# Second block of a three-block model: two PSUM banks and buffers for the attention's turned probabilities and results, the scan in two banks with its products grouped by kind, three of the head norms placed between attention tiles

## Chip, cores and metric

The kernel runs on one core of one Trainium2 chip. The metric is device time in microseconds of one execution; lower is better.

## The reference

Three transformer blocks follow each other on a sequence of 512 positions of width 1024. Only the mixing of the second block is touched. It is, shortened:

```
h = rmsnorm(x, attn_norm); p_nsa, p_rw, p_moba = split(h @ w_in)
o_nsa  = head_rmsnorm(nsa_mixer(p_nsa), nsa_out_gain)     # 6 heads of 64: compressed, selected and window attention, gated
o_rw   = rwkv7_mixer(p_rw)                                # 4 heads of 64: a linear recurrence with a 64x64 state per head
o_moba = head_rmsnorm(moba_mixer(p_moba), moba_out_gain)  # 6 heads of 64: attention over chosen blocks
x = x + concat(o_nsa, o_rw, o_moba) @ w_out
```

`head_rmsnorm` divides each head's 64 numbers by their root mean square and multiplies by a gain.

## The kernel before, in words

Every activation lies in SBUF with features on the 128 partitions and tokens along them, so that 128 features are a tile of 128 x 512. Weights come in units of 1024 x 128. TensorE multiplies them in three passes (line 573), because ScalarE and VectorE split each weight unit and each input into a high and a low part.

The work is written as stages. Each stage is a set of generators, one for each engine, and each generator yields a planned time before it issues a few instructions. `weave` merges the generators of an engine by these times, so the planned times fix the order of instructions in each engine's queue, and semaphores do the rest. Planned times are in units; a unit of the plan is the time of one weight unit. A stage's time that comes earlier or later in the plan changes only the order.

In the second block 26 units of projections (`Projected`, two lines of 17 and 9 units) fill the tiles P2. A unit's result stands in PSUM bank 6 or 7, and VectorE evicts it (line 962). Beside and after them run:

- `PairCausal`, the attention of both kinds. Its 36 steps each treat one tile of 128 queries for a pair of heads (m = 0, 1), against up to four tiles of 128 keys. The first 24 steps belong to the first attention (two steps to a result tile), the other 12 to the second (one step to a result tile), in all 24 result tiles. A step: scores on TensorE (line 1696) into banks 0 and 1; mask and minimum on VectorE (line 1753); exponential on ScalarE (line 1777); reciprocal and scaling on VectorE (lines 1760 to 1764); a turn for each m, in which TensorE transposes the probabilities in tiles of 128 x 128 into bank 2 (line 1713) and ScalarE copies them to the buffer PT (line 1785); weighing of the values on TensorE (line 1724, line 1728 for the compressed part, whose probabilities are turned by line 1711 and copied by line 1787) into bank 3; and after a tile's last step a copy of the result by ScalarE (line 1792). Bank 2 and PT are single, or one half for each m: the second turn waits for the first copy, the copies of a step wait for the weighing of the step before.
- `RwkvScan`, the recurrence in 16 chunks of 32 positions, a chunk each 1.45 units, from unit 26.4. The positions of chunk c lie on the 32 partitions (c mod 4). A chunk's products, for four heads each: x from the tokens (line 1425) and from the state (line 1445), VectorE's copy with a minus sign (line 1492), u (line 1458), its copy (line 1496), the state's increment (lines 1452 and 1467) and the state's update on VectorE (lines 1488 and 1500), and the result from state (line 1429), tokens (line 1430) and u (line 1434), copied by ScalarE (line 1509). The result's products from state and tokens alternate head by head, two heads before and two after the second half of the state's increment. x stands in banks 4 and 5, u in 4, the state's increment in bank 6, the result in bank 7.
- `RwkvOutput`, after the scan, normalises its result (lines 1812 to 1845).
- `HeadMeans`, six norms of a 128 x 512 tile of attention results: a square on ScalarE (line 1870), a product with a matrix of ones on TensorE (line 1891), logarithm and exponential on ScalarE (lines 1879 and 1880), each with a table load ahead of it, and a product on VectorE (line 1898). All six are planned after the scan, from 1.5 units after it on, 0.3 units apart, with two buffers and banks 4 and 5.

After them the output projection of the block begins, again with line 573, and needs all norms.

The two lines that give the order of turns and copies in the plan before:

```
x.turned = [max([x.after[0] + 0.12] + ([last.keep[1] + 0.08, last.out + 0.05] if s else []))]
x.turned.append(max(x.after[1] + 0.12, x.keep[0] + 0.08))
```

Of the kernel before, what the change touches and what calls it, by code (L numbers as in the profile page):

```python
# [41 lines left out]
CH = 32  # L42

# [892 lines left out]
class Projected(Line):  # L936


    def __init__(self, core, n, at, dst, func=ACT.Copy, bias=None, inputs=None, before=None, sums=None, eighth=()):
        super().__init__(core, n, at, WHOLE, (6, 7), inputs)  # L940
# [453 lines left out]
class RwkvScan(Stage):  # L1394
# [17 lines left out]
    def tensor(self, pe):  # L1412
# [23 lines left out]
        yield self.when(0) - 0.3  # L1436
        pe.wait_ge(self.rwkv.kept.sem, self.rwkv.kept.at(12))
        pe.wait_ge(self.compress.kept.sem, self.compress.kept.at(2))
        x_first(0)
        for c in range(n):  # L1440
            t0, d = self.when(c), self.step
            yield t0
            pe.wait_ge(self.s_kept.sem, self.s_kept.at(c + 1))
            for h, (lo, t, o, r) in enumerate(heads):
                last = pe.matmul(x_bank(c, h, t), AR[lo:lo + 64, t, c, 0], STATE[lo:lo + 64, c % 2, t], start=False, stop=(t == 1))
            last.then_inc(self.x_ready.sem, 1)
            if c:
                out_last(c - 1)
            if c == 0:
                pe.wait_ge(self.proj.free.sem, self.proj.free.at(N2))  # L1450
            for lo, t, o, r in heads:
                pe.matmul(s_bank(lo, t), tok(c)[1][:, o:o + 64], tok(c)[2][:, o:o + 64], start=(t == 0), stop=False)
            yield t0 + 0.33 * d
# [2098 lines left out]
```

## Time and profile before

| what | value |
|---|---|
| median of 3 runs | 2953.69 us (2952.72 to 2962.31) |
| profiled execution, its own time | 2959.89 us |
| its span, first to last instruction | 2958.1 us |
| mean granted TensorE clock | 0.928 of full speed |
| TensorE busy | 2768.2 us, 94% |
| VectorE busy | 1521.9 us, 51% |
| ScalarE busy | 1058.2 us, 36% |
| GpSimd busy | 313.1 us, 11% |

Busy times are of one profiled execution. TensorE's products are pipelined and their ends are modelled, so the step from one start to the next tells more than the duration of one. The granted clock has two levels, 1.2 and 2.4 GHz, shown as 0.5 and 1; a mean between them is a share of time at each.

### The profile page before, as it was taken

The numbers are of one execution on the slowest core, as the hardware profiler recorded it, in microseconds if no ns is written. First come the engines' busy times: TensorE is split into PE (matmuls) and PEld (weight loads), VectorE is DVE, ScalarE is ACT, GpSimd is POOL, SyncE is SP. The second block draws the span as 40 slices with busy tenths as digits, with TensorE's granted clock in tenths as the row PEclk, the third lists the DMA queues.
The fourth block names the chain that finished last, engine by engine and source line by source line (L and its number), as shares of the span: only waits on it lengthen the run. The fifth ranks groups of instructions, "written<-read, shape, count | busy, mean of one in ns | idle before, by whom it ended". The sixth has DMA issues, their size and how long they took to land.

```text
span 2958.1 us, 36434 instructions
## 1 busy us (share of the span) xinstructions
PE 2768.2 (94%) x14774; PEld 2203.9 (75%) x14774; DVE 1521.9 (51%) x2473; ACT 1058.2 (36%) x1831; POOL 313.1 (11%) x220
## 2 busy tenths in 40 slices
PE   7999999999999999988869999998899899899998
PEld 6778888999997767655636777776666568678886
DVE  3786643544445463733334787544753453533444
ACT  3365444442223332322264222343332332322322
POOL 0043210012220100000001222020000000100001
PEclk8999999999999999955568999999989999999999
DMA  3211111223332413200003665332121123223332
GB/s 117 72 44 51 58 58 58 74 84 93 93 93 93 136 57 101 77 1 1 1 1 100 199 199 188 97 118 68 58 64 57 36 62 95 86 86 93 95 98 71
DMA packets 70852, 239.06 MB, mean 81 GB/s; under 512 B 12212, under 2 KB 13109, under 8 KB 70430
## 3 DMA queue, kind: packets, MB, share of 16 engines
q1 hardware_dynamic: 63054, 208.88, 23.0%
q10 hardware_dynamic: 7632, 27.86, 2.8%
q8 instruction: 118, 1.93, 0.3%
q14 instruction: 48, 0.39, 0.0%
HBM read 234.06 MB, written 2.64 MB: 80 GB/s over the span
## 4 chain that ended last, share of the span: by engine, by line
PE 62%; DVE 11%; ACT 4%; issue 3%; POOL 1%; ACTq 0%; DVEq 0%; POOLq 0%
PE ps L573 49%; DVE wl L364 2%; PE ps L1713 1%; PE ps L2656 1%; PE ps L1696 1%; ACT wh L358 1%; PE ps L1724 1%; PE ps L3307 1%; DVE xl L654 1%; DVE arena L3000 1%; PE ps L1429 1%; DVE arena L1032 1%; PE ps L1430 1%; PE ps L1572 0%; ACT arena L1785 0%
## 5 line engine op out<-in xcount | busy, mean ns | idle before, releaser
L573 PE MATMUL ps<-xh,wh 128*128 128x512 f32 (+1 forms) x2728 | 1022.8, 389 | 39.0 <-DVE xl L679 14.8
L573 PE MATMUL ps<-xl,wh 128*128 128x512 f32 (+1 forms) x2728 | 995.5, 379 | 0.0
L573 PE MATMUL ps<-xh,wl 128*128 128x512 f32 (+1 forms) x2728 | 991.4, 378 | 0.0
L364 DVE TENSOR_TENSOR wl<-ring,wh 128x1024 fp32r<-128x1024 f32 x374 | 471.1, 1260 | 657.0 <-ACT wh L358 655.9
L358 ACT ACTIVATE wh<-ring 128x1024 fp32r<-128x1024 f32 x374 | 395.3, 1057 | 998.8 <-PE ps L573 891.1
L573 PEld LDWEIGHTS ps<-xh,wh 128*128 128x128 f32 x2728 | 504.6, 191 | 179.7 <-issue 56.8
L573 PEld LDWEIGHTS ps<-xl,wh 128*128 128x128 f32 x2728 | 503.0, 190 | 101.2 <-issue 9.6
L573 PEld LDWEIGHTS ps<-xh,wl 128*128 128x128 f32 x2728 | 504.2, 191 | 99.4
L734 POOL TENSOR_TENSOR arena<-arena 128x512 f32<-128x512 f32 (+1 forms) x42 | 72.0, 1721 | 1899.2 <-ACT arena L718 1899.2
L1952 PE MATMUL ps<-xh,wh 128*128 128x264 f32 (+1 forms) x816 | 260.1, 319 | 9.6 <-DVE xl L423 9.6
L1952 PE MATMUL ps<-xh,wl 128*128 128x264 f32 (+1 forms) x816 | 234.9, 288 | 0.0
L1952 PE MATMUL ps<-xl,wh 128*128 128x264 f32 (+1 forms) x816 | 234.9, 288 | 0.0
L1952 PEld LDWEIGHTS ps<-xh,wh 128*128 128x128 f32 x816 | 157.3, 193 | 38.4 <-issue 20.7
L1952 PEld LDWEIGHTS ps<-xl,wh 128*128 128x128 f32 x816 | 158.3, 194 | 1.0
L1952 PEld LDWEIGHTS ps<-xh,wl 128*128 128x128 f32 x816 | 157.9, 194 | 0.0
L818 DVE TENSOR_TENSOR h<-ps,h 128x512 f32<-128x512 f32 (+1 forms) x64 | 44.3, 692 | 155.6 <-PE ps L573 155.6
L875 POOL TENSOR_TENSOR arena<-arena 128x516 f32<-128x516 f32 (+1 forms) x44 | 81.0, 1842 | 217.5 <-ACT arena L854 217.5
L862 ACT ACTIVATE arena<-arena 128x512 f32<-128x512 f32 x44 | 27.8, 632 | 203.2 <-DVE arena L894 203.2
L1753 DVE CUSTOM_DVE_ANT_0 arena<-ps,con 128x128 f32<-128x128 f32 (+3 forms) x72 | 33.2, 488 | 115.8 <-PE ps L1696 84.1
L820 DVE SCALAR_TENSOR_TENSOR h<-ps,mod,h 128x512 f32<-128x512 f32 x40 | 30.0, 751 | 113.5 <-PE ps L573 113.5
L1713 PE MATMUL ps<-con,arena 128*128 128x128 f32 x180 | 52.0, 409 | 31.7 <-ACT arena L1785 22.3
L878 POOL TENSOR_TENSOR arena<-arena 128x512 f32<-128x512 f32 x44 | 58.4, 1327 | 159.4 <-ACT arena L862 159.4
(391 smaller groups left out, 3010.8 us busy)
## 6 DMA issues: line engine op xcount, KB each, us to landing
ring<-in_weights SPq DMA_DIRECT2D x374, 512.0 KB, 3.6
arena<-in_w_ada ACTq DMA_DIRECT2D x48, 512.0 KB, 4.6
arena<-in_cmp_w SPq DMA_DIRECT2D x2, 2048.0 KB
h<-in_x ACTq DMA_DIRECT2D x4, 528.0 KB, 6.6
arena<-strip_scratch SPq DMA_DIRECT2D x8, 264.0 KB, 3.7
out_features<-arena SPq DMA_DIRECT2D x8, 256.0 KB, 2.1
con<-in_consts SPq DMA_DIRECT2D x1, 777.0 KB, 11.0
arena<-in_c ACTq DMA_DIRECT2D x1, 512.0 KB, 3.8
```

The lines of the kernel that those rows point to most:

```text
L358: act.activation(flat(self.wh[:, s % 2]), flat(self.ring[:, s % RING]), ACT.Copy).then_inc(self.hi_ready, 1)
L364: dve.tensor_tensor(flat(self.wl[:, s % 2]), flat(self.ring[:, s % RING]), flat(self.wh[:, s % 2]).bitcast(F32), ALU.subtract).then_inc(se ...
L573: last = pe.matmul(self.place(u, e), w[:, k, :], x[:, k, o:o + m], start=(k == 0 and i == 0), stop=(k == self.chunks - 1 and i == 2))
L654: ins = dve.tensor_tensor(xl, a, xh, ALU.subtract)
L734: pool.tensor_tensor(self.acc, self.sq[:, 0] if k == 1 else self.acc, self.sq[:, k % 2], ALU.add).then_inc(self.added.sem, 1)
L818: ins = dve.tensor_tensor(out, self.got(u), out, ALU.add)
L820: ins = dve.scalar_tensor_tensor(out=out, in0=self.got(u), scalar=self.scale[u], in1=out, op0=ALU.mult, op1=ALU.add)
L875: pool.tensor_tensor(g, g, self.r_gate, ALU.mult).then_inc(self.gate_scaled.sem, 1)
L878: pool.tensor_tensor(self.mid[:, j, 2], self.mid[:, j, 2], self.r, ALU.mult).then_inc(self.scaled.sem, 1)
L1713: last = pe.transpose(ps[:, 2, j * P:(j + 1) * P], self.X[:, s % 3, m, j * P:(j + 1) * P], ident)
L1753: dve.tensor_tensor_reduce(out=self.X[:, s % 3, m, 0:nk], in0=core.ps[:, m, 0:nk], in1=core.c("causal")[:, DIAG - x.i * P:DIAG - x.i * P + ...
L1952: last = pe.matmul(self.place(e), w[:, k, :], x[:, k, o:o + m], start=(k == 0 and n == 0), stop=(k == NC - 1 and n == 2))
```

## The change

Five edits in one:

1. The attention's turned probabilities stand in bank 2 for m = 0 and in bank 6 for m = 1, and PT has two buffers, one for even and one for odd steps (the second on the tiles MV and MV + 1). The second turn no longer waits for the first copy; the copies of step s wait for the weighing of step s - 2. The plan puts both turns before both copies.
2. Result tiles alternate between banks 3 and 7.
3. The scan uses banks 4 and 5 alone and starts at unit 26.6. x of each chunk is made in one visit, both kinds; the state's increment is one run of products after u; the result is one run of products after it, by kind (tokens, u, state). x waits for ScalarE's copy of the result before. The copy of x is two instructions. Its plan has other shares of the chunk.
4. The norms of the first attention are planned right after their tiles, in bank 7, those of the second from 1.8 units after the scan's end on in bank 5, at least 0.8 units apart, with one buffer each for square and root (on the tiles NG and MV + 2). Result tiles 5, 9 and 13 wait for the logarithm of a norm.
5. The second line of projections uses banks 5 and 4.

```diff
+SCAN_STEP = 1.45
...
-        x_bank = lambda c, h, t: core.ps[rows(c), 4 + h % 2, t * 64:t * 64 + 64]
-        s_bank = lambda lo, t: core.ps[lo:lo + 64, 6, 256 + t * 64:256 + t * 64 + 64]
-        o_bank = lambda c, lo, t: core.ps[lo:lo + 64, 7, t * CH:(t + 1) * CH]
+        x_bank = lambda c, h, t: core.ps[rows(c), 4 + h % 2, 256 * (h % 2) + 64 * t:256 * (h % 2) + 64 * t + 64]
+        u_bank = lambda c, r: core.ps[rows(c), 4, 64 * r:64 * r + 64]
+        s_bank = lambda lo, t: core.ps[lo:lo + 64, 4, 256 + t * 64:256 + t * 64 + 64]
+        o_bank = lambda lo, t: core.ps[lo:lo + 64, 5, t * CH:(t + 1) * CH]
...
-        def out_first(c, some):
-            for lo, t, o, r in some:
-                pe.matmul(o_bank(c, lo, t), STATE[lo:lo + 64, c % 2, t], AR[lo:lo + 64, t, c, 1], start=(t == 0), stop=False)
-                pe.matmul(o_bank(c, lo, t), tok(c)[2][:, o:o + 64], parts(c)[:, r, 1, 1], start=False, stop=False)
-
-        def out_last(c):
+        def state(c):
+
+            for e, F in ((1, lambda o, r: tok(c)[2][:, o:o + 64]), (0, lambda o, r: U[rows(c), 64 * r:64 * r + 64])):
+                for lo, t, o, r in heads:
+                    last = pe.matmul(s_bank(lo, t), tok(c)[e][:, o:o + 64], F(o, r), start=(e == 1 and t == 0), stop=(e == 0 and t == 1))
+            last.then_inc(self.s_ready.sem, 1)
+
+        def out(c):
             for lo, t, o, r in heads:
-                last = pe.matmul(o_bank(c, lo, t), U[rows(c), 64 * r:64 * r + 64], parts(c)[:, r, 0, 1], start=False, stop=(t == 1))
+                pe.matmul(o_bank(lo, t), tok(c)[2][:, o:o + 64], parts(c)[:, r, 1, 1], start=(t == 0), stop=False)
+            for lo, t, o, r in heads:
+                pe.matmul(o_bank(lo, t), U[rows(c), 64 * r:64 * r + 64], parts(c)[:, r, 0, 1], start=False, stop=False)
+            for lo, t, o, r in heads:
+                last = pe.matmul(o_bank(lo, t), STATE[lo:lo + 64, c % 2, t], AR[lo:lo + 64, t, c, 1], start=False, stop=(t == 1))
             last.then_inc(self.o_ready.sem, 1)
...
             pe.wait_ge(self.s_kept.sem, self.s_kept.at(c + 1))
+            if c:
+                pe.wait_ge(self.o_kept.sem, self.o_kept.at(c))
+            else:
+                pe.wait_ge(self.rwkv.kept.sem, self.rwkv.kept.at(12))
+                pe.wait_ge(self.proj.free.sem, self.proj.free.at(N2))
+            x_first(c)
...
-            dve.tensor_scalar(self.X[rows(c)].rearrange("p (o n) -> p o n", o=2), core.ps[rows(c), 4:6, 0:128], -1.0, None,
-                              ALU.mult).then_inc(self.x_kept.sem, 1)
+            for e in range(2):
+                ins = dve.tensor_scalar(self.X[rows(c), 128 * e:128 * e + 128], core.ps[rows(c), 4 + e, 256 * e:256 * e + 128], -1.0, None,
+                                        ALU.mult)
+            ins.then_inc(self.x_kept.sem, 1)
...
-            x.turned = [max([x.after[0] + 0.12] + ([last.keep[1] + 0.08, last.out + 0.05] if s else []))]
-            x.keep = [x.turned[0] + 0.1]
-            x.turned.append(max(x.after[1] + 0.12, x.keep[0] + 0.08))
-            x.keep.append(x.turned[1] + 0.1)
-            x.weigh = x.keep[1] + 0.1
+            x.turned = [max([x.after[0] + 0.12] + ([last.keep[0] + 0.08] if s else []))]
+            x.turned.append(max([x.after[1] + 0.12, x.turned[0] + 0.06] + ([last.keep[1] + 0.08] if s else [])))
+            x.keep = [max(x.turned[0] + 0.12, last.keep[1] + 0.04 if s else 0)]
+            x.keep.append(max(x.turned[1] + 0.12, x.keep[0] + 0.08))
+            x.weigh = max(x.keep[1] + 0.14, last.weigh + 0.05 if s else 0)
...
+    def bank(self, s):
+        return 3 + 4 * (self.tiles[s] % 2)
+
+    def room_for(self, pe, s):
+        t = self.tiles[s]
+        if t >= 2:
+            pe.wait_ge(self.out_used.sem, self.out_used.at(t - 1))
+        if t in (5, 9, 13):
+            pe.wait_ge(self.means.logs.sem, self.means.logs.at(t // 4))
...
-            if s or m:
-                pe.wait_ge(self.kept.sem, self.kept.at(2 * s + m))
-            else:
+            if s:
+                pe.wait_ge(self.kept.sem, self.kept.at(2 * s + m - 1))
+            elif m == 0:
                 self.room(pe)
...
-                last = pe.transpose(ps[:, 2, j * P:(j + 1) * P], self.X[:, s % 3, m, j * P:(j + 1) * P], ident)
+                last = pe.transpose(ps[:, 2 + 4 * m, j * P:(j + 1) * P], self.X[:, s % 3, m, j * P:(j + 1) * P], ident)
...
-                if s:
-                    act.wait_ge(self.weighed.sem, self.weighed.at(s))
-                else:
+                if s >= 2:
+                    act.wait_ge(self.weighed.sem, self.weighed.at(s - 1))
+                elif s == 0:
                     self.room_kept(act)
-                ins = act.activation(self.PT[:, m, 0:nk], ps[:, 2, 0:nk], ACT.Copy)
+                ins = act.activation(self.PT[s % 2][:, m, 0:nk], ps[:, 2 + 4 * m, 0:nk], ACT.Copy)
...
+        for n, (t, x, gain, ready, bank, room) in enumerate(self.items):
+            yield t
+            ready(act)
+            if n:
+                act.wait_ge(self.summed.sem, self.summed.at(n))
+            act.activation(self.sq, x, ACT.Square).then_inc(self.squared.sem, 1)
+            yield t + 0.4
+            act.wait_ge(self.summed.sem, self.summed.at(n + 1))
+            if n:
+                act.wait_ge(self.applied.sem, self.applied.at(n))
+            act.activation(self.r, core.ps[:, bank, :], ACT.Ln, bias=core.c("eps6"), scale=1.0 / 64).then_inc(self.logs.sem, 1)
+            act.wait_ge(self.logs.sem, self.logs.at(n + 1))
+            act.activation(self.r, self.r, ACT.Exp, scale=-0.5).then_inc(self.root.sem, 1)
...
-    PT = core.area(NKC * T, 2, T)
+    PT = [core.area(t * T, 2, T) for t in (NKC, MV)]
...
-                               eighth=[a - u + t for a in (NQ, MQ) for t in range(3)]))
+                               eighth=[a - u + t for a in (NQ, MQ) for t in range(3)], banks=(5, 4) if u else (6, 7)))
...
-        free = max(free + 0.3, x.out + 0.1)
+        free = max(free + 0.8, x.out + 0.02 if n < 3 else max(x.out + 0.1, scanned + 1.8))
```

## Rows read from the trace of the kernel before

**Rows 1.** Stage windows: us, busy time of each engine, granted clock, DMA share
```profile
1250.00:1496.00 246.00, 221.26 (x1589) 148.02 (x1587) 81.38 (x308) 63.83 (x201) 0.00 (x0) 0.53 0.01 3
...
1504.60:1541.20 36.60, 17.58 (x64) 8.38 (x64) 11.78 (x33) 33.91 (x49) 0.00 (x0) 0.72 0.00 0
```
**Rows 2.** TensorE's groups by line, 1250 to 1496 us: busy, mean ns, idle before
```profile
L1713 PE MATMUL ps<-con,arena 128*128 128x128 f32 x136 | 40.9, 425 | 8.6 <-ACT arena L1785 6.2 <-DVE arena L1762 2.4
L1696 PE MATMUL ps<-arena 64*128 64x384 f32 (+3 forms) x108 | 39.7, 835 | 0.0
L1724 PE MATMUL ps<-arena 128*64 128x128 f32 x276 | 36.7, 431 | 7.7 <-ACT arena L1785 4.0 <-ACT arena L1787 3.7
L1429 PE MATMUL ps<-arena 64*64 64x32 f32 x128 | 25.6, 290 | 0.8 <-ACT arena L1509 0.8
L1430 PE MATMUL ps<-arena 32*64 32x32 f32 x128 | 25.4, 287 | 0.0
...
L1434 PE MATMUL ps<-arena 32*64 32x32 f32 x128 | 10.0, 290 | 0.0
```
**Rows 3.** Waits, 1250 to 1496 us: us in total, times, longest us
```profile
PE ps L1713 <- ACT arena L1785: 6.2, 9, 0.8
...
ACT arena L1509 <- PE ps L1434: 5.0, 3, 3.8
PE ps L1724 <- ACT arena L1785: 4.0, 8, 0.7
PE ps L1724 <- ACT arena L1787: 3.7, 5, 0.9
```
**Rows 4.** Timeline of TensorE in two chunks of the scan: start us, us, instructions
```profile
1382.27 0.42 PE L1429 MATMUL ps<-arena 64*64 64x32 f32 x2
1382.62 0.41 PE L1430 MATMUL ps<-arena 32*64 32x32 f32 x2
...
1383.65 1.06 PE L1425 MATMUL ps<-arena 32*32 32x64 f32 x8
...
1387.11 0.64 PE L1445 MATMUL ps<-arena 64*32 64x64 f32 x8
1387.68 0.32 PE L1434 MATMUL ps<-arena 32*64 32x32 f32 x2
...
1388.32 0.69 PE L1724 MATMUL ps<-arena 128*64 128x128 f32 x4
...
1396.38 0.69 PE L1467 MATMUL ps<-arena 32*64 32x64 f32 x8
1397.00 0.42 PE L1429 MATMUL ps<-arena 64*64 64x32 f32 x2
```
**Rows 5.** Timeline of TensorE's weight loads at a change of shape
```profile
1258.90 0.51 PEld L1467 LDWEIGHTS ps<-arena 32*64 32x64 f32 x8 [0.33 <-issue]
```
**Rows 6.** Timeline of VectorE in the scan
```profile
1436.83 0.41 DVE L1492 TENSOR_SCALAR arena<-ps 32x256 f32<-32x256 f32 x1
```
**Rows 7.** Timeline of ScalarE in the head norms
```profile
1516.43 1.28 ACT L1879 ACT_TABLE_LOAD   x1
...
1519.74 0.63 ACT L1880 ACTIVATE arena<-arena 128x512 f32<-128x512 f32 x1
...
1521.29 1.28 ACT L1879 ACT_TABLE_LOAD   x1
```
**Rows 8.** Timeline of TensorE in the head norms
```profile
1525.77 1.93 PE L1891 MATMUL ps<-arena,con 128*128 128x512 f32 x2
```
**Rows 9.** Timeline of TensorE at the first instruction of projection unit 17
```profile
1180.13 0.50 PE L573 MATMUL ps<-xh,wh 128*128 128x512 f32 x1 [1.17 <-DVE arena L962]
```
**Rows 10.** A window of six microseconds, columns as in rows 1
```profile
1276.00:1282.00 6.00, 4.83 (x44) 3.55 (x42) 3.49 (x12) 2.54 (x6) 0.00 (x0) 0.78 0.00 0
```
**Rows 11.** Timeline of TensorE: weighing at two clocks
```profile
1407.65 1.55 PE L1724 MATMUL ps<-arena 128*64 128x128 f32 x12
...
1500.36 0.88 PE L1724 MATMUL ps<-arena 128*64 128x128 f32 x12 [0.58 <-ACT arena L1785]
```

More of the change, by code:

```diff
@@ L1446, in tensor @@
             last.then_inc(self.x_ready.sem, 1)
[L1447 to L1453, printed above, removed]
+            yield t0 + 0.25 * d
             if c == 0:
@@ L1718, in weigh @@
             self.values_ready(pe, s)
-            if x.begins and self.tiles[s]:
-                pe.wait_ge(self.out_used.sem, self.out_used.at(self.tiles[s]))
-            out = [ps[64 * m:64 * m + 64, 3, 0:P] for m in range(2)]
+            if x.begins:
+                self.room_for(pe, s)
+            out = [ps[64 * m:64 * m + 64, self.bank(s), 0:P] for m in range(2)]
             for j in range(x.i + 1):
                 for m in range(2):
-                    last = pe.matmul(out[m], x.values[m][:, j], self.PT[:, m, j * P:(j + 1) * P], start=(x.begins and j == 0),
+                    last = pe.matmul(out[m], x.values[m][:, j], self.PT[s % 2][:, m, j * P:(j + 1) * P], start=(x.begins and j == 0),
                                      stop=(x.ends and j == x.i))
@@ L1848, with __init__ @@
 class HeadMeans(Stage):
-    def __init__(self, core, items, before, tmp):
-        self.core, self.items, self.before = core, items, before
+    def __init__(self, core, items, sq, r):
+        self.core, self.items, self.sq, self.r = core, items, sq, r
         n = len(items)
-        self.sq, self.r = core.area(tmp, 2, SEQ), core.area(tmp + 2 * SEQ, 2, SEQ)
-        self.squared, self.summed, self.root, self.applied = (core.take(a, n) for a in (
-            "mean_squared", "mean_summed", "mean_root", "mean_applied"))
+        self.squared, self.summed, self.logs, self.root, self.applied = (core.take(a, n) for a in (
+            "mean_squared", "mean_summed", "mean_logs", "mean_root", "mean_applied"))
     def ready(self, eng, n):
@@ L1881, in scalar @@
-        yield from zipped(squares(), roots())
-    def tensor(self, pe):
-        for n, (t, x, gain, ready) in enumerate(self.items):
-            yield t + 0.15
-            if n >= 2:
-                pe.wait_ge(self.root.sem, self.root.at(n - 1))
-            else:
-                pe.wait_ge(self.before.root.sem, self.before.root.at(2))
+        for n, (t, x, gain, ready, bank, room) in enumerate(self.items):
[11 more added lines that the diff above has]
+            act.activation(self.r, self.r, ACT.Exp, scale=-0.5).then_inc(self.root.sem, 1)
@@ L1890, in tensor @@
+    def tensor(self, pe):
+        for n, (t, x, gain, ready, bank, room) in enumerate(self.items):
+            yield t + 0.18
+            room(pe)
+            if n:
+                pe.wait_ge(self.logs.sem, self.logs.at(n))
             pe.wait_ge(self.squared.sem, self.squared.at(n + 1))
-            pe.matmul(self.core.ps[:, 4 + n % 2, :], self.core.c("pair64"), self.sq[:, n % 2], start=True, stop=True).then_inc(
-                self.summed.sem, 1)
+            pe.matmul(self.core.ps[:, bank, :], self.core.c("pair64"), self.sq, start=True, stop=True).then_inc(self.summed.sem, 1)
@@ L1894, in vector @@
     def vector(self, dve):
-        for n, (t, x, gain, ready) in enumerate(self.items):
-            yield t + 0.55
+        for n, (t, x, gain, ready, bank, room) in enumerate(self.items):
+            yield t + 0.65
             dve.wait_ge(self.root.sem, self.root.at(n + 1))
-            dve.scalar_tensor_tensor(out=x, in0=x, scalar=gain, in1=self.r[:, n % 2], op0=ALU.mult, op1=ALU.mult).then_inc(
-                self.applied.sem, 1)
+            dve.scalar_tensor_tensor(out=x, in0=x, scalar=gain, in1=self.r, op0=ALU.mult, op1=ALU.mult).then_inc(self.applied.sem, 1)
```

93 lines of the change are left out of this document (36 added, 57 removed).

## The prediction

> **What bounds the kernel now.** I first looked for the place where TensorE's granted clock falls, since the whole run has 0.93. Stage windows over it [rows 1] show the second block's mixing after its projections: from 1250 to 1496 us TensorE is busy 221.3 of 246 us at a granted clock of 0.53, which is nearly always the lower of its two levels (1.2 against 2.4 GHz), while VectorE works 33% and ScalarE 26% of the time. From 1504.6 to 1541.2 us the picture turns: ScalarE is busy 33.9 of 36.6 us and TensorE half of them. These are two stretches with two limits.
>
> In the first, TensorE's own queue sets the pace. The grouped lines [rows 2] show what it does: transposes, scores and weighing of the attention (lines 1713, 1696, 1724: 117 us together), and the scan's small products, where lines 1429 and 1430 stand out with 25.6 and 25.4 us. Line 1434 makes as many products of the same output width in 10.0 us. The rest of the stretch is idle time [rows 3]: 6.2 us where the second turn of a step (line 1713) waits for ScalarE's copy of the first, and 7.7 us where weighing (line 1724) waits for ScalarE's last copies.
>
> **Part 1, the scan's products grouped.** The order in time of two chunks [rows 4] gives the pitch of each group. Line 1429 (64 rows by 64 columns of the array) and line 1430 (32 rows by 64) alternate head by head: 0.35 us from one pair of instructions to the next, 1.38 us for two heads, 2.76 us for the four of a chunk. A group of four heads of one kind takes 0.62 us (line 1467), lines 1434 and 1452 together 0.64 us. Lines 1425, 1445 and 1458 stay as they are, so they drop out. What changes costs 2.76 + 0.62 + 0.64 = 4.02 us a chunk.
>
> Afterwards no group changes its shape inside. State update and the two 32-row kinds of the result become runs of 16 instructions. Of the 0.62 us of eight such instructions, 0.33 is the gap that the weight loads show where the shape changes [rows 5]; so I charge 0.33 + 2 x 0.29 = 0.91 us for each run, and for the four products with the state, now one run of 64 rows, the 0.57 us of line 1445 in rows 4. Sum 2.39 us: 1.63 less a chunk, **26 us** for 16. Bounds: if each eight instructions keep their whole 0.62, the sum is 3.05 and the saving 16 us; if 16 cost the 0.64 of lines 1434 and 1452, it is 1.85 and 35 us.
>
> The Trainium skill, "TensorEngine Tiling (Array Packing)", section "Tiling Modes", says that changing the tiling mode drains the engine. By that, the trace agrees: 0.17 us an instruction where the shape alternates, 0.08 inside a run. Yet the Trainium skill's "TensorE: Matmul & The Clock Gate", section on packing small matmuls, speaks against the full saving: a weight load overlaps running products only where its row group differs. Lines 1434 and 1452 belong to neighbouring chunks, which lie on different partitions, and each new run lies on one chunk's; by that rule the saving would be the end with 16 us.
>
> The copy of x becomes two VectorE instructions of 128 columns for one of 256, which takes 0.41 us [rows 6]. It is hidden: the chain of one chunk is three groups of products of a microsecond or so, three VectorE steps of 0.4 to 0.5 and their delays, about 7 us, and a chunk has 246/16 = 15.4 us now and some 13 after. Without that cover it would cost at most another 0.41 x 16 = 7 us.
>
> A new wait stands in front of each chunk: x now shares bank 5 with the result, so TensorE waits there for ScalarE's copy (line 1509), and all of the attention is queued behind it. The plan sets the copy a quarter of a step ahead, some 3 us, on an engine three quarters idle: 0, bound 0.5 us a chunk.
>
> **Part 2, two banks and two buffers.** The second turn no longer waits for the first copy (6.2 us). Weighing still needs the last copy (7.7 us), but the plan gives it 0.14 units, not 0.1, and the next step's turns may stand between. I take the first and half of the second, **10 us**; bounds 4 and 14. Late in the block, where steps are a chain, the last two gain the 0.8 us that stands between their turns [rows 3]: 1.6 us.
>
> **Part 3, head norms between tiles.** On ScalarE a norm takes 4.86 us from its first table load to the next norm's, of which 3.9 us are loads, logarithm and exponential without a break [rows 7]. Five follow each other. Three leave a stretch that ScalarE bounds: 14.6 us, of which I give back 2.6 because square and root now have one buffer each and follow in series: **-12 us**. They arrive in the stretch that TensorE bounds. A norm's product costs 1.9 us at the lower clock [rows 8], 5.7 us for three, and each closes ScalarE for 3.9 us to the copies that TensorE waits for. TensorE has the scan and other steps in between, so I charge 1.5 us each, 4.5 us (bounds 0 and 11.7). Bank 7's next tile waits for the logarithm, planned about a unit earlier, some 10 us: 0. Net **-2 us**; bounds -6 and +5.
>
> **Part 4, projections.** Unit 17 moves to bank 5; before, it waited 1.2 us for the eviction of unit 16 from the bank that both used [rows 9]: **-1.2 us**.
>
> **Clock.** A clock of 0.53 means 6% of 246 us at the upper level, 15 us, in short pieces such as 1276 to 1282 us [rows 10]. Twelve weighings take 0.88 us there and 1.55 at the lower level [rows 11]. Wide products now stand closer together, so I take as much again: 15 us, in which 0.4 is gained, **-6 us**; bounds 0 and -15.
>
> Sum: -26 - 10 - 1.6 - 2 - 1.2 - 6 = -46.8 us. From the profiled execution (time 2959.9, span 2958.1) that leads to 2913; the median of the runs shown is 6.2 lower, 2953.7, and the forecast is **2907 us**.
>
> **Rivals.** (a) *The relief is swallowed.* TensorE ends each piece sooner and then waits for the other engines. For it: 24.7 us of idle are there already. Against: their loads of 26 and 33%, and a chain of 7 us in a chunk of 15. The saving would be the low ends, 16 + 4 + 1.6 + 1.2 with part 3 at +5 and nothing from the clock: 18 us, 2936. (b) *The clock opens.* If half of the 117 us of attention products ran at the upper level, they would shed 0.43 of their time, 25 us in place of the 6 counted: 2888; all of them, 50 us: 2863. For it: the pieces that rows 10 show. Against: nearly all of 246 us at 90% busy stayed at the lower level. (c) *Slower: the new wait for the copy of the result.* If ScalarE were late in each chunk by a norm's 3.9 us, 62 us would be lost against 47 gained: 2969. It decides from 2.9 us a chunk. Against it: that copy waited for TensorE, 3.8 us at the longest [rows 3], and not TensorE for it. (d) *Nothing:* if the 0.35 us of a pair were the price of small products and not of the change of shape, part 1 would vanish; with part 2 at 4 and part 3 at +5 the time stays within 5 us. Line 1467's 0.62 us for four heads speaks against it directly.
>
> **Chances.** The forecast as summed (30 to 65 us less) 0.60; (a) 0.17; (b) 0.12; (c) 0.05; (d) 0.06. A measurement of this kernel can tell about 0.3% from no change, 9 us. Faster by more than that 0.89, within it 0.06, slower 0.05. The range reaches from the near half of (b) to (a) and leaves out (c) and (d): **2868 to 2938 us**.
>
> **What would show it.** In the profile after: lines of the result's products at 8 to 12 us each, not 25; chunks some 13 us apart; no transposes of a second turn that wait for ScalarE; three of the logarithms between 1290 and 1430 us; a ScalarE-bound stretch of some 24 us; a clock between 0.53 and 0.6 in the stretch. I would be wrong if a run of 16 products cost much more than 0.9 us, if TensorE's idle time grew past 40 us, or if the clock rose above 0.65.

## The result, and the profile after

The changed kernel takes 2909.92 us (median, 2904.41 to 2920.64), the kernel before on the same chip 2955.78 us. The ratio is 0.9846, 95% interval 0.9812 to 0.988: faster by 45.9 us by the medians, and by 35.5 to 55.6 us by the interval. The forecast was 2907, range 2868 to 2938.

Stage windows of the profile after, columns as in [rows 1]: the scan stretch, the ScalarE-bound stretch behind it, and the stretch from the copy of the first result tile to that of the nineteenth, which I use for comparisons below:

```profile
1250.00:1457.00 207.00, 183.70 (x1493) 123.74 (x1490) 79.62 (x308) 73.39 (x202) 0.00 (x0) 0.53 0.00 1
...
1468.35:1491.30 22.95, 12.40 (x50) 6.00 (x50) 8.74 (x25) 20.00 (x31) 0.00 (x0) 0.64 0.00 1
...
1229.70:1465.02 235.32, 208.97 (x1670) 140.36 (x1672) 90.88 (x345) 84.80 (x234) 0.00 (x0) 0.56 0.01 3
```

The last of these stretches in the kernel before:

```profile
1241.68:1501.29 259.61, 232.42 (x1661) 154.82 (x1663) 87.38 (x324) 69.82 (x218) 0.00 (x0) 0.55 0.01 3
```

So the same tiles come 24.3 us sooner, nearly all of it busy time of TensorE (232.4 to 209.0 us); its idle time stays (27.2 and 26.3 us). From there to the first product of the output projection it is 63.2 us before and 49.2 after. The first window, 207 us where [rows 1] have 246, does not hold the same work (1493 of TensorE's instructions for 1589), so it flatters the change; the stretch between the two copies has nearly as many in both (1670 and 1661) and is the fair one. The ScalarE-bound window takes 23 us where they have 36.6, with two head norms in it for five.

TensorE's groups by line, 1250 to 1457 us, beside [rows 2]:

```profile
L1719 PE MATMUL ps<-con,arena 128*128 128x128 f32 x125 | 36.0, 420 | 9.7 <-DVE arena L1768 7.7 <-DVE arena L1770 1.9
...
L1442 PE MATMUL ps<-arena 64*64 64x32 f32 x120 | 9.1, 287 | 0.0
L1440 PE MATMUL ps<-arena 32*64 32x32 f32 x120 | 8.8, 280 | 0.0
L1438 PE MATMUL ps<-arena 32*64 32x32 f32 x120 | 8.7, 278 | 0.0
```

The result's products from state (now line 1442) and tokens (1438) fell from 25 us a line to 9, with nearly the same mean of one: what went is the time that alternating took. The turns (line 1719) no longer wait for ScalarE, but wait more for VectorE than before.

TensorE's waits in the stretch of 235 us, beside [rows 3]:

```profile
PE ps L1719 <- DVE arena L1768: 10.0, 9, 2.3
PE ps L1730 <- ACT arena L1791: 4.2, 7, 0.7
PE ps L1433 <- DVE arena L1493: 4.0, 5, 1.1
PE ps L1730 <- ACT arena L1793: 3.0, 4, 0.9
PE ps L1462 <- DVE arena L1488: 2.4, 3, 1.4
PE ps L1719 <- DVE arena L1770: 1.9, 2, 1.0
```

None of them is for the copy of the scan's result (line 1506), the wait of rival (c). One chunk on TensorE's timeline, beside [rows 4], the increment's run first:

```profile
1352.81 1.12 PE L1433 MATMUL ps<-arena 32*64 32x64 f32 x16
1353.86 0.69 PE L1730 MATMUL ps<-arena 128*64 128x128 f32 x4
...
1356.66 0.64 PE L1438 MATMUL ps<-arena 32*64 32x32 f32 x8
1357.11 0.62 PE L1440 MATMUL ps<-arena 32*64 32x32 f32 x8
1357.66 0.64 PE L1442 MATMUL ps<-arena 64*64 64x32 f32 x8
1358.23 0.47 PE L1719 MATMUL ps<-con,arena 128*128 128x128 f32 x1
```

From start to start, the increment's run of 16 takes 1.05 us, the result's run of 16 with 32 rows 1.00 us, its eight with 64 rows 0.57. That is 2.62 us a chunk where the forecast has 2.39 and the kernel before 4.02.

### The profile page after: what moved, and what is told of

The parts are those of the page before. It is cut to its first block, busy times and chain, and to the rows that moved or that the text cites. A ratio compares the mean times of both kernels' runs of the same rounds, so it can differ in the third digit from the quotient of the medians.

```text
span 2910.2 us, 36469 instructions
## 1 busy us (share of the span) xinstructions
PE 2730.5 (94%) x14774; PEld 2181.1 (75%) x14774; DVE 1523.2 (52%) x2489; ACT 1059.5 (36%) x1831; POOL 312.4 (11%) x220
## 4 chain that ended last, share of the span: by engine, by line
PE 62%; DVE 11%; ACT 4%; issue 3%; POOL 1%; ACTq 0%; DVEq 0%; POOLq 0%
PE ps L574 50%; DVE wl L365 2%; PE ps L2653 1%; PE ps L1719 1%; ACT wh L359 1%; PE ps L1730 1%; PE ps L1703 1%; PE ps L3314 1%; DVE xl L655 1%; DVE arena L3007 1%; DVE arena L1033 1%; PE ps L1433 0%; PE ps L1569 0%; POOL arena L735 0%; DVE xl L653 0%
## 5 line engine op out<-in xcount | busy, mean ns | idle before, releaser
L574 PE MATMUL ps<-xh,wh 128*128 128x512 f32 (+1 forms) x2728 | 1021.8, 389 | 37.7 <-DVE xl L680 14.6
L655 DVE TENSOR_TENSOR xl<-arena,xh 128x512 fp32r<-128x512 f32 (+1 forms) x108 | 72.1, 725 | 14.1 <-ACT xh L645 14.1
```

The source lines that it names most:

```text
L574: last = pe.matmul(self.place(u, e), w[:, k, :], x[:, k, o:o + m], start=(k == 0 and i == 0), stop=(k == self.chunks - 1 and i == 2))
L655: ins = dve.tensor_tensor(xl, a, xh, ALU.subtract)
```

## The experiments

Each profile is cut at four events of the second block: the eviction of projection unit 16, the copies of the first and of the nineteenth result tile, and the first product of the output projection. Unit 16 lies ahead of the change; all that the change and the experiments touch lies between the first and the last event, so this cut leaves out the noise of the rest of the program, which no edit touches and which takes 2560.7 to 2575.7 us in these 14 executions. Each row is one execution, so how much a block varies by itself is not known; its first part, up to tile 1, is 60.2 to 60.4 us in seven of the kernels. Times in us; "busy, idle, clock" are TensorE's in the scan stretch, that is from the first to the nineteenth copy; medians and ratios come from separate timings, each against the kernel before on the same chip.

| kernel | block | up to tile 1 | scan stretch | tail | busy / idle | clock | median, ratio (95%) |
|---|---|---|---|---|---|---|---|
| before | 385.1 | 62.3 | 259.6 | 63.2 | 232.4 / 27.2 | 0.55 | 2955.78 |
| changed | 344.8 | 60.3 | 235.3 | 49.2 | 209.0 / 26.3 | 0.56 | 2909.92, 0.9846 (0.9812 to 0.988) |
| e1_group_only | 366.6 | 63.9 | 239.9 | 62.8 | 204.9 / 35.0 | 0.56 | 2939.33, 0.9944 (0.9931 to 0.9956) |
| e2_alternate | 375.4 | 60.3 | 265.9 | 49.2 | 241.3 / 24.6 | 0.54 | 2941.89, 0.9943 (0.9924 to 0.9962) |
| e3_one_bank | 366.6 | 61.1 | 253.0 | 52.6 | 216.9 / 36.1 | 0.54 | 2933.75, 0.9928 (0.9916 to 0.9941) |
| e4_norms_last | 342.2 | 60.4 | 221.1 | 60.7 | 197.0 / 24.1 | 0.59 | 2909.07, 0.9846 (0.9833 to 0.986) |
| e5_joint_tables | 331.6 | 60.3 | 231.5 | 39.8 | 206.6 / 25.0 | 0.57 | 2895.86, 0.9803 (0.9765 to 0.9841) |
| e6_step_1_3 | 348.9 | 60.3 | 246.2 | 42.4 | 216.0 / 30.2 | 0.56 | 2917.18, 0.9876 (0.984 to 0.9911) |
| e7_step_1_6 | 337.8 | 60.2 | 223.1 | 54.5 | 201.8 / 21.3 | 0.56 | 2912.04, 0.9851 (0.9817 to 0.9884) |
| e8_turns_later | 329.9 | 63.7 | 220.6 | 45.6 | 201.6 / 19.0 | 0.58 | 2897.63, 0.9796 (0.9761 to 0.9831) |
| e9_tables_turns | 315.5 | 60.9 | 221.6 | 33.0 | 205.5 / 16.1 | 0.57 | 2882.71, 0.9757 (0.9736 to 0.9778) |
| e10_and_norms_last | 317.2 | 60.9 | 218.2 | 38.1 | 202.8 / 15.4 | 0.55 | 2879.80, 0.9749 (0.9728 to 0.9769) |
| e11_one_result_bank | 349.5 | 60.3 | 240.4 | 48.8 | 216.2 / 24.2 | 0.53 | 2911.86, 0.9869 (0.9845 to 0.9893) |
| e12_one_turn_bank | 362.6 | 61.0 | 249.3 | 52.3 | 212.1 / 37.2 | 0.56 | 2926.35, 0.9908 (0.9886 to 0.9929) |

The kernel before was timed beside each group of runs, at 2955.78 us for the changed kernel, 2955.25 for e1 to e4, 2955.13 for e5 to e8 and 2951.34 for e9 to e12. None of the experiments leaves out part of the computation.

**e1_group_only.** The kernel before with the scan's products grouped, and nothing else.

```diff
-            if c:
-                out_last(c - 1)
...
-            out_first(c, heads[0:2])
...
-            out_first(c, heads[2:4])
+            out(c)
```

> The kernel before with the grouping alone: state increment in one run after u, result in one run by kind after it, banks 6 and 7 as before, attention and norms as before. The forecast's part 1 stands for 26 us less than before. Theory A (the groups cost what the profile of the changed kernel shows, 2.62 us for 4.02 in a chunk, and TensorE sets the pace): 22 us less, some 2933, and the stretch from the eviction of unit 16 to the first output product 363 us for 385. Theory B (the time saved on TensorE turns into waits for the other engines, and the second banks were needed to use it): less than 10 us gained, the idle time of TensorE in the scan well above 25 us.

The block is 18.5 us shorter and the time 15.9 less by the medians, 16.5 by the ratio (0.56%). That lies between the two theories, 22 and less than 10: the block of 366.6 us is nearer to theory A's 363, and TensorE's idle time of 35.0 us is theory B's sign. Where the rest went stands in the table: TensorE is busy 27.5 us less in the scan stretch and idle 7.8 us more. Its waits there:

```profile
PE ps L1707 <- DVE arena L1756: 8.2, 6, 1.9
PE ps L1707 <- ACT arena L1779: 6.4, 10, 0.8
...
PE ps L1459 <- DVE arena L1490: 3.6, 3, 1.3
```

The turns (line 1707, before 1713) waited 3.6 us for VectorE's scaling in the kernel before and now 8.2; the wait for u's copy was 1.9 us and is now 3.6. Part of the relief became waits for VectorE.

**e2_alternate.** The changed kernel with the result's products alternating head by head again; the rest, the single run of 16 for the increment too, stays.

```diff
             for lo, t, o, r in heads:
-                pe.matmul(o_bank(lo, t), tok(c)[2][:, o:o + 64], parts(c)[:, r, 1, 1], start=(t == 0), stop=False)
+                pe.matmul(o_bank(lo, t), STATE[lo:lo + 64, c % 2, t], AR[lo:lo + 64, t, c, 1], start=(t == 0), stop=False)
+                pe.matmul(o_bank(lo, t), tok(c)[2][:, o:o + 64], parts(c)[:, r, 1, 1], start=False, stop=False)
...
```

> The changed kernel with one thing undone: the result's products with the state and with the tokens alternate head by head again, the rest of the order as changed. Theory A (a change of the array's shape costs 0.35 us for each pair): 3.3 us for 1.57 in a chunk, 1.7 x 16 = 28 us more than the changed kernel, some 2937. Theory B (TensorE has slack in the changed kernel, because its 23 us of idle come from chains): under half of that, 14 us or less.

The scan stretch is 30.6 us longer, the time 29 more by the ratios (0.97%): theory A. Timeline of TensorE and, below it, what the two lines cost in 1240 to 1480 us:

```profile
1365.11 0.42 PE L1438 MATMUL ps<-arena 64*64 64x32 f32 x2
1365.45 0.41 PE L1439 MATMUL ps<-arena 32*64 32x32 f32 x2
1365.80 0.42 PE L1438 MATMUL ps<-arena 64*64 64x32 f32 x2
```

```profile
L1438 PE MATMUL ps<-arena 64*64 64x32 f32 x115 | 23.7, 297 | 0.0
L1439 PE MATMUL ps<-arena 32*64 32x32 f32 x114 | 23.2, 294 | 0.0
```

The 0.35 us from pair to pair is back, and with it the price of before. The order inside the result's visit carries this part; the visit's new place in the chunk alone does not. One rival is that it was not the change of shape but of the rows used. The run of line 1442 speaks against it: it goes from one half of the rows to the other at every head, in one shape, and its eight instructions still take 0.57 us.

**e3_one_bank, e11_one_result_bank, e12_one_turn_bank.** These split the attention's second banks and buffers. e3 has bank 3 alone for results, bank 2 and one buffer PT for the turned probabilities, and the plan of before for turns and copies; e12 has only the latter two; e11 only the first.

```diff
# e3 and e11
     def bank(self, s):
-        return 3 + 4 * (self.tiles[s] % 2)
+        return 3
# e3 and e12
-                last = pe.transpose(ps[:, 2 + 4 * m, j * P:(j + 1) * P], self.X[:, s % 3, m, j * P:(j + 1) * P], ident)
+                last = pe.transpose(ps[:, 2, j * P:(j + 1) * P], self.X[:, s % 3, m, j * P:(j + 1) * P], ident)
...
-                ins = act.activation(self.PT[s % 2][:, m, 0:nk], ps[:, 2 + 4 * m, 0:nk], ACT.Copy)
+                ins = act.activation(self.PT[0][:, m, 0:nk], ps[:, 2, 0:nk], ACT.Copy)
```

> The changed kernel with the attention's second bank for turned probabilities, second buffer and second result bank undone, order and waits of the turns as before; scan, norms and projections as changed. The forecast's part 2 is worth 10 + 1.6 us, so 2921. Theory A (two banks remove ScalarE's waits and the same time comes back as waits for VectorE): 0 to 5 us more than the changed kernel, and TensorE's waits for ScalarE back at some 14 us with those for VectorE back at some 7. Theory B (the second banks are what lets the grouping pay): 15 us more or above.

> Edit: the changed kernel with the turned probabilities in one bank and one buffer, with the planned times of the kernel before for turns and copies, and the result in two banks. It differs from e3_one_bank (2933.8) in the result's banks alone. Theory A, as above: 8 us or more below e3_one_bank, 2925 or less. Theory B: 2930 to 2936, with the waits of the second group's turns for ScalarE's copy as in e3_one_bank (5.5 us in the scan stretch) and longer waits for the copies before the weighing (9.9 us).

> Edit: the changed kernel with the attention's result in bank 3 alone, so that a tile's products wait until ScalarE copied the result before. The turned probabilities keep two banks and two buffers. Theory A, the result's second bank carries what the second banks gave beyond the forecast (17.7 us in the scan stretch in e3_one_bank, forecast 10): 8 us or more over the changed kernel, with a wait of the weighing products or of their first for the copy of the result. Theory B, the turned probabilities' bank and buffer carry it: 0 to 4 us more.

e3 is 24 us slower than the changed kernel, twice the forecast's 11.6, and its block 21.8 longer; by its size that is theory B. Theory A's exchange is not seen: TensorE's waits for ScalarE are back at 15.4 us in e3's scan stretch, but those for the scaled probabilities are 11.5 us there and 11.9 in the changed kernel. They came mostly with the grouping (5.0 us before, 9.6 in e1), not with the second banks. e12 came out between its two theories (2926.35) and has the waits that its theory B names, but its block is only 4.0 us shorter than e3's, and e11's 4.7 longer than the changed kernel's: the result's bank carries 4 to 5 us in the traces, the turned probabilities 17. In the timings e11 is not to be told from the changed kernel (2 us by the medians, 6.8 by the ratios, whose intervals overlap), so I count the 4 to 5 as likely, not as shown; by the medians that is theory B for e11, and the wait for the copy of the result that theory A names is not there. TensorE's waits in the scan stretch of e12:

```profile
PE ps L1719 <- DVE arena L1768: 9.0, 9, 2.0
PE ps L1719 <- ACT arena L1791: 5.5, 9, 0.8
PE ps L1730 <- ACT arena L1793: 5.2, 7, 0.9
PE ps L1433 <- DVE arena L1493: 5.0, 6, 1.3
PE ps L1730 <- ACT arena L1791: 4.9, 8, 0.7
```

Against the changed kernel, the second turn's wait for ScalarE (5.5 us) is back and those ahead of the weighing are 10.1 us, not 7.2. These 8.4 us are most of the 10.9 us of idle time between the two. The tail adds 3.1 us. In e3 another 7.9 us of the 17.7 in its scan stretch is busy time, at a clock of 0.54 for 0.56; in e11 7.2 us, at 0.53, with no new wait at all, so nothing in e11's trace ties its 4.7 us to the bank.

**e4_norms_last.** The changed kernel with all six norms after the scan, in bank 5, with its single buffers for square and root and 0.7 units apart. It tests the placing alone and not the kernel before's two buffers.

```diff
-            free = max(free + 0.8, x.out + 0.02 if n < 3 else max(x.out + 0.1, scanned + 1.8))
+            free = max(free + 0.7, x.out + 0.1, scanned + 1.8)
```

> The changed kernel with all six head norms after the scan, in bank 5, one after the other; nothing else changed. The forecast's part 3 nets 2 us. Theory A (three norms in the attention cost their product, 5.6 us, and almost nothing by ScalarE's tables): the scan's stretch is 6 us shorter, the last stretch 14 us longer, so 8 us more than the changed kernel, some 2918. Theory B (each norm's 3.9 us on ScalarE stop the attention): no more than 2 us more, or less than the changed kernel, with a scan stretch 12 us shorter.

Theory B: the time is the same within 1 us. The trace shows how: the tail is 11.5 us longer without the change's placing, and the scan stretch 14.2 shorter, 12.0 of them busy time. The products of the three norms are 6 us of that (some 2.04 us each at the lower clock); the clock is 0.59 against 0.56.

**e5_joint_tables.** The profile after shows what a norm costs at the block's end, on ScalarE's timeline, as [rows 7] did:

```profile
1507.96 1.28 ACT L1879 ACT_TABLE_LOAD   x1
1510.16 0.69 ACT L1879 ACTIVATE arena<-ps,con 128x512 f32<-128x512 f32 x1 [0.93 <-PE ps L1890]
1510.87 1.28 ACT L1881 ACT_TABLE_LOAD   x1
1512.16 0.63 ACT L1881 ACTIVATE arena<-arena 128x512 f32<-128x512 f32 x1
```

Each logarithm and each exponential of the six norms and of the RWKV branch's gate has a table load ahead of it, 16 in the block. The Trainium skill, "ScalarE: Activation LUTs", section "Table sets: the hidden batching unit", says that one table set holds both functions, so that a logarithm and an exponential need one load. The trace disagrees for the code as it was built, with two loads of 1.28 us each for a norm; the experiment asks for the joint set once by hand, ahead of the block's first exponential.

```diff
         flat = self.X.rearrange("p m i q c -> p (m i q c)")
+        self.core.exp_ln(act)
         act.activation(flat, flat, ACT.Exp).then_inc(self.exps.sem, 1)
```

> Edit: the table set that holds both the exponential and the logarithm is loaded once before the second block's compressed branch, so that the 16 table loads of 1.28 us each, at the logarithms and exponentials of the RWKV branch's gate and of the six head norms, go. Theory A, ScalarE's chain sets the end of the block after the scan and takes part in the scan stretch: the tail from the copy of result tile 18 to the first output projection is 8 to 11 us shorter than the changed kernel's 49, the scan stretch up to 6 shorter, together about 15 less, near 2895. Theory B, ScalarE isn't what limits: about 3 less than the changed kernel (2907), with the table loads gone from the trace and TensorE's idle time in the tail unchanged at about 22 of 57 us.

Theory A: 2895.86 us where it had 2895. The intervals of this ratio and the changed kernel's overlap (0.9841 and 0.9812), so the trace has to carry it: the block is 13.2 us shorter, the tail 9.4 and the scan stretch 3.8, and TensorE's idle time in the tail is 12.8 us, not 21.5. ScalarE's timeline at the end of the block:

```profile
1503.38 0.63 ACT L1875 ACTIVATE arena<-arena 128x512 f32<-128x512 f32 x1
1506.24 0.69 ACT L1880 ACTIVATE arena<-ps,con 128x512 f32<-128x512 f32 x1 [2.23 <-PE ps L1891]
1506.96 0.63 ACT L1882 ACTIVATE arena<-arena 128x512 f32<-128x512 f32 x1
```

With one load for the block, the 16 of 1.28 us are gone, and what stands between square and logarithm is TensorE's product. This alone is worth more than the placing of the norms.

**e6_step_1_3, e7_step_1_6.** The chunks' planned distance, 1.45 units in both kernels.

```diff
-SCAN_STEP = 1.45
+SCAN_STEP = 1.3     # e6; 1.6 in e7
```

> Edit: the scan's chunks are planned 1.3 units of the branch's time apart, where the changed kernel has 1.15 or near it, so the scan ends later and more chunks lie in the tail. Theory A, TensorE's total work sets the time and the tail has idle time that chunks can fill: a few us less than the changed kernel, 2905. Theory B, the gate's and the last norms' chain at the end sets it: within 5 us, 2910 to 2915.

> Edit: the scan's chunks are planned 1.6 units apart. Theory A, TensorE's total work sets the time and the idle 22 of 57 us in the tail can be filled: up to 8 us less than the changed kernel, 2902. Theory B, the chain at the end sets it: the last norms and the gate start later, the block ends 5 to 20 us later, 2915 to 2930.

The first expectation names a wrong starting value: the changed kernel has 1.45, not 1.15, so e6 plans the chunks closer and its scan ends earlier. Read so, e6 shows a denser plan: the scan stretch is 10.9 us longer, the tail 6.8 us shorter, the block 4.1 longer and the median 7.3 us higher, above both of its theories. e7 has the block 7.0 us shorter (scan stretch -12.2, tail +5.3), but a median 2 us higher, between its theories. These stretches do not hold the same work, since chunks move from one to the other (1675, 1670 and 1617 of TensorE's instructions in the scan stretch of e6, the changed kernel and e7). Over both stretches TensorE idles 47.0 us in e6, 47.8 in the changed kernel and 45.3 in e7, so spreading the scan fills hardly any idle time; most of the difference is busy time. The timing doesn't bear e7's 7 us out, and neither theory is settled.

**e8_turns_later.** The turns planned a tenth of a unit later, so that scaling on VectorE has more time.

```diff
-            x.turned = [max([x.after[0] + 0.12] + ([last.keep[0] + 0.08] if s else []))]
-            x.turned.append(max([x.after[1] + 0.12, x.turned[0] + 0.06] + ([last.keep[1] + 0.08] if s else [])))
+            x.turned = [max([x.after[0] + 0.22] + ([last.keep[0] + 0.08] if s else []))]
+            x.turned.append(max([x.after[1] + 0.22, x.turned[0] + 0.06] + ([last.keep[1] + 0.08] if s else [])))
```

> Edit: the turns of the probabilities are planned 0.1 unit later, so that TensorE has other work between the scores and the turns while VectorE scales. Theory A, the 12 us in which TensorE's turns wait for VectorE's scaling (10.0 and 1.9 us in the scan stretch) come from the order in the queue: those waits fall below 5 us and the time by up to 8, near 2903. Theory B, the tiles' chain or the scan's is what TensorE waits for, and another wait takes their place: 0 to 5 us more than the changed kernel.

Theory A. Window and waits of the scan stretch:

```profile
1239.35:1459.93 220.58, 201.63 (x1670) 135.22 (x1671) 91.93 (x347) 83.74 (x234) 0.00 (x0) 0.58 0.01 4
```

```profile
PE ps L1462 <- DVE arena L1488: 4.5, 4, 1.4
PE ps L1730 <- ACT arena L1791: 3.6, 6, 0.9
PE ps L1719 <- DVE arena L1768: 3.0, 3, 2.2
...
PE ps L1717 <- DVE arena L1768: 1.3, 2, 0.8
PE ps L1719 <- DVE arena L1770: 1.2, 2, 0.8
```

The waits for the scaled probabilities fell from 11.9 to 5.5 us, a little above the 5 expected. The stretch lost 14.7 us: 7.4 idle and 7.3 busy, at a clock of 0.58 for 0.56. Some of that is a shift, since the stretch ahead of it is 3.4 us longer; the tail is 3.6 us shorter. The median is 12 us lower where up to 8 was expected; the intervals of the two ratios overlap a little, the block in the trace is 14.9 us shorter. So it is the order in the queue that made TensorE wait for the scaled probabilities; VectorE's load is 42% there. The wait for the copy of x (line 1462) grew from 2.4 to 4.5 us in their place.

**e9_tables_turns, e10_and_norms_last.** Both finds together, and then with the norms last as in e4.

> Edit: the changed kernel with both edits of the runs before, the joint table set loaded once (2895.9 alone) and the turns planned 0.1 unit later (2897.6 alone), where the changed kernel is 2909.9. Theory A, the two act at different places (the table loads in the tail, 9.4 of 13.2 us there; the waits for VectorE's scaling in the scan stretch, 14.7 us): they add up, 2897.6 + 2895.9 - 2909.9 = 2884, and TensorE's waits for the scaled probabilities stay below 6 us in the scan stretch. Theory B, they relieve the same chain: 2892 or more.

> Edit: as e9_tables_turns, and all six head norms lie after the scan, where the changed kernel has three of them between the tiles. Theory A, the table loads made the late norms dear (six norms with two loads of 1.28 us each are 15.4 us of ScalarE at the end of the block), so that without them the norms between the tiles cost more (14.2 us in the scan stretch in e4_norms_last) than they save in the tail (11.5 us less up to 3 loads pairs of 7.7): 5 to 8 us less than e9_tables_turns. Theory B, placing is neutral as before: within 3 us of e9_tables_turns.

e9 takes 2882.71 us (2884 by its ratio, applied to the kernel before's 2955.78) where adding up gave 2884: theory A. It is 2.4% faster than the kernel before, and its interval lies wholly below that of the changed kernel. Tail and block of e9's trace, from the copy of the nineteenth tile and from the eviction of unit 16 to the first product of the output projection:

```profile
1493.67 0.76 PE L574 MATMUL ps<-xh,wh 128*128 128x512 f32 x1 [2.78 <-DVE xl L655]
```

```profile
1460.66:1493.67 33.01, 21.48 (x110) 10.20 (x111) 16.05 (x48) 20.95 (x52) 0.00 (x0) 0.79 0.00 0
1178.15:1493.67 315.52, 284.73 (x2079) 192.24 (x2079) 157.41 (x482) 118.02 (x317) 0.00 (x0) 0.68 0.07 19
```

The block is 29.3 us shorter than the changed kernel's; e5's 13.2 and e8's 14.9 make 28.1. So the trace shows the addition too, for the block as a whole: the tail is 16.2 us shorter where the two edits alone have 13.0, the scan stretch 13.7 where they have 18.5. TensorE's waits for the scaled probabilities are 3.0 us. e10 is the same as e9 within 3 us (2879.80 us; block 317.2 for 315.5), theory B: with the loads gone the placing of the norms is still neutral, now with 3.4 us less in the scan stretch against 5.1 more in the tail, where it was 14.2 against 11.5.

## Why the prediction was right, point by point

The mechanism was right, a queue of TensorE that sheds changes of shape and waits; that the total came within a microsecond of the sum (45.9 us for 46.8) is in part luck. The interval of the ratio is 20 us wide. In the two traces the block, all that the change touches, is 40.3 us shorter; the spans differ by 47.9, because the stretch ahead of the block is 10.0 us shorter and the one behind it 2.4 longer. And the terms missed in opposite directions. The experiments, one trace each, split the 40.3 us: 18.5 come with the grouping (e1, forecast 26) and 21.8 with the attention's second banks and buffers (e3, forecast 11.6). What else the change does lies between e1 and e3, which both have a block of 366.6 us: nothing in sum, where parts 3 and 4 and the clock were to bring 9.2.

- **Part 1, 26 us.** Right in mechanism, too large for the edit alone. The pitches give 4.02 - 2.62 = 1.40 us a chunk, 22 us, since a run of 16 takes 1.0 to 1.05 us and not 0.91. The mis-sized step is "0.33 + 2 x 0.29": each two instructions of a run are one product, and in the trace after one product starts 0.11 us behind the other (line 1433), so that eight make some 0.85 us and the change of shape adds about 0.2, not 0.33. TensorE's busy time fell by 27.5 us in e1, 5 more than the pitches explain, but 7.8 came back as waits, above all for VectorE, and the time fell by 16. This is rival (a), at work on more than a quarter of the relief. The change of shape as the cause is shown by e2. A run of 16 lies between the 0.91 charged and the 1.24 of twice a group of eight, and a little nearer to the first: 1.24 counts the change of shape twice. The Trainium skill, "TensorE: Matmul & The Clock Gate", section on packing small matmuls, says that a weight load overlaps running products only where its row group differs. It gives no 1.24; that was the prediction's working. The trace agrees with it for these products: 0.11 us from one to the next on the same 32 rows, 0.05 on two sets of them (the last section).
- **Part 2, 10 us and 1.6 late.** The undersized step is "I take the first and half of the second, 10 us". Undoing it cost 24 us in time and 21.8 in the block. As idle time it was right: 9.8 us between e3 and the changed kernel in the scan stretch, where 5.5 of the second turn's wait went and 2.7 ahead of the weighing. What the term lacked is the busy time, 7.9 us more in e3 at a clock of 0.54 for 0.56, and 3.4 us in the tail, where it had 1.6.
- **Part 3, net -2 us.** Tail -11.5, scan stretch +14.2 for +10.2. e4 has single buffers too, so the tail's term to compare is the 14.6 us and not the 12 that are left after the buffers; those were not tried by themselves. Between e1 and e3, where more differs, the tail is 10.2 us shorter and the scan stretch 13.1 longer. Net +2.7 in the trace and +0.9 in time, inside the bounds. Products are 6.1 us for the 5.7 counted. The closed ScalarE did not show as waits: idle time rose by 2.2 us and not 4.5, and the rest is busy time, beside a lower clock.
- **Part 4, -1.2 us.** No experiment undoes it alone. The first product of unit 17 no longer waits, as TensorE's timeline shows in place of [rows 9]:

```profile
1168.86 0.50 PE L574 MATMUL ps<-xh,wh 128*128 128x512 f32 x1
1169.20 0.39 PE L574 MATMUL ps<-xl,wh 128*128 128x512 f32 x1
```

- **Clock, -6 us.** As a term of the total it hardly came: 0.55 to 0.56 in the comparison stretch. (The 0.88 us of [rows 11] stand at 1500 us, where the clock is at its upper level, not in the window of [rows 10].) It acted inside the parts (0.53 to 0.59 over the experiments) and in both directions.
- **The new wait, 0.** No wait for the copy of the scan's result appears; rival (c) is out. Rival (b) is out too, since the clock stayed at 0.53 in the window of 207 us. Rival (d) falls with e2.
- **The copy of x, hidden.** TensorE's wait for it (line 1488) is 2.4 us for 1.7 before; the charge of nothing held within a microsecond.
- **Signs.** The result's lines came at 9 us, a chunk each 13.6 us (217.4 us from the first product of the first chunk to ScalarE's copy of the last chunk's result, over 16), the ScalarE-bound stretch at 23 us, the clock at 0.53, idle time at 26 us. Logarithms stand at 1284.8, 1347.0 and 1418.4 us, the first 5 us ahead of the named window.

## What to carry to other kernels

Group small products by the rows and columns of the array that they use before anything else is tuned: 127 fewer changes of shape took 27.5 us off TensorE's busy time in e1, 0.22 us each, and 104 more added 32.3 us in e2, 0.31 each. Then read the waits again, since over a quarter of the 27.5 came back as waits, mostly for VectorE, which is 36% busy there. Here such waits were in part a matter of the order in the queue: a tenth of a unit in the plan (e8) moved 12 us in time and 15 in the block, where the second result bank moved 4.7 in the block and the placing of the norms 2.7. And set against a sum the time of the part that the change touches as well as the whole: here the total agreed to a microsecond, and its parts missed by 7.5, 10 and 9 us. Look at what stands between the useful instructions of an engine that bounds a stretch: 16 table loads that one load can replace were worth 14 us.

## What the runs showed of the hardware

**The clock moves time in stretches that no edit touches.** From the first output product of the second block to the end, the changed kernel and e8 have the same instructions:

```profile
1514.18:2910.20 1396.02, 1321.99 (x5456) 1024.58 (x5456) 724.43 (x901) 449.23 (x588) 120.16 (x75) 0.97 0.31 99
```

```profile
1505.48:2890.60 1385.12, 1311.02 (x5456) 1019.22 (x5456) 724.34 (x901) 449.34 (x588) 120.80 (x75) 0.98 0.32 100
```

The 10.9 us are TensorE's busy time (11.0 us), beside another granted clock. Between 1000 and 1060 us, ahead of the block, the kernel before has 0.89 and the changed one 1.00, and its unit 16 is evicted 10.0 us earlier (1169.38 for 1179.40), with the same projections ahead of it. In the 12 experiments that eviction starts at 1175.6 to 1182.2 us, so it is the changed kernel's execution that stands apart. So two profiled executions can differ by some 10 us ahead of the block and by 11 behind it for reasons outside the change, and a part worth less than that must be read from its own stretch. What makes the clock fall at one place or another was not settled.

**Less waiting often came with less busy time.** Where waits of TensorE went, its busy time in the same stretch mostly fell too, for the same products: 7.3 us beside 7.4 us of idle time in e8, 7.9 beside 9.8 from e3 to the changed kernel. From e12 to the changed kernel it is only 3.1 beside 10.9, and e11 is against a simple rule: 2.1 us less idle time than the changed kernel, 7.2 more busy time, clock 0.53.

**A run has a price per instruction that shape does not set alone.** Sixteen instructions of 32 rows on the same partitions take 1.05 us in the changed kernel, eight and eight on neighbouring chunks' partitions 0.64 in the kernel before [rows 4], both at the lower clock. TensorE's timeline of the kernel before shows the two lines interleaved, though all of line 1434's stand ahead of line 1452's in TensorE's program:

```profile
1387.80 0.30 PE L1434 MATMUL ps<-arena 32*64 32x32 f32 x2
1387.86 0.32 PE L1452 MATMUL ps<-arena 32*64 32x64 f32 x2
1387.91 0.30 PE L1434 MATMUL ps<-arena 32*64 32x32 f32 x2
1387.97 0.32 PE L1452 MATMUL ps<-arena 32*64 32x64 f32 x2
```

Each line alone keeps the 0.11 us from product to product, and the two go side by side. That the other partitions are the cause was not tried by itself, and with 64 rows it does not show: line 1442 goes between the halves of the rows and has 0.11 us as well. Grouping gave this overlap up: line 1452's products now stand in one run with line 1467's, on one chunk's partitions.
